# A hybrid decoder step on one core: recurrent stage reordered, loops written out, first convolution tap on ScalarE

## What is computed

```python
u = x @ w_in
gate_branch, rec = u[..., :D_RNN], u[..., D_RNN:]
xc = causal_dwconv(concat([conv_buf, rec]), conv_w, conv_b)   # width 4
r = sigmoid(block_diag(xc, w_a, b_a)); i = sigmoid(block_diag(xc, w_x, b_x))
log_a = -RG_C * r * softplus(-lam)
a, mult = exp(log_a), sqrt(-expm1(2.0 * log_a))
h = scan(h[t] = a[t] * h[t-1] + mult * i * xc)
y = (h * gelu(gate_branch)) @ w_out
```

## Time and profile before

| | us |
|---|---|
| median of 3 executions | 2996.12 (2994.41 to 3001.76) |
| profiled execution, its own time | 2997.21 |
| its span, first to last instruction | 2995.4 |
| granted TensorE clock, mean over the span | 0.955 of full speed |
| PE busy, DVE busy, POOL busy, ACT busy | 2764.8, 1695.7, 867.5, 519.7 |

### The profile page before, as it was taken

The page is one execution under the profiler, slowest core; times in us unless marked ns, Lnnn a source line. Parts: engine busy times, 40 slices in busy tenths (PEclk is TensorE's granted clock), DMA queues, the critical chain, the costliest instruction groups (busy, mean ns, idle before and its releaser), DMA issues. The chain is left out here.

```text
span 2995.4 us, 42944 instructions
## 1 busy us (share of the span) xinstructions
PE 2764.8 (92%) x16822; PEld 2682.6 (90%) x16822; DVE 1695.7 (57%) x2451; ACT 519.7 (17%) x841; POOL 867.5 (29%) x672
## 2 busy tenths in 40 slices
PE   6797999999999999999998888879999999999996
PEld 5697999999999999989996767779999999999995
DVE  7666366555556556731315656654765556555666
ACT  4335020000000000210103444431100000000001
POOL 2334233333333333323231010013333333333331
PEclk9899999999999999999997787879999999999998
DMA  5511111111111111123112212121111111111111
GB/s 140 88 49 56 37 43 43 49 44 43 43 43 50 43 43 43 56 93 129 72 56 85 82 67 88 39 99 43 43 50 43 43 43 43 49 44 43 43 50 64
DMA packets 44760, 174.04 MB, mean 58 GB/s; under 512 B 5205, under 2 KB 5781, under 8 KB 44214
## 3 DMA queue, kind: packets, MB, share of 16 engines
q1 hardware_dynamic: 39442, 143.08, 14.1%
q10 hardware_dynamic: 5156, 28.58, 3.4%
HBM read 140.20 MB, written 23.05 MB: 55 GB/s over the span
## 5 line engine op out<-in xcount | busy, mean ns | idle before, releaser
L591 PE MATMUL psum<-xn_hi,w_hi 128*128 128x352 f32 x3648 | 799.0, 327 | 70.3 <-DVE xn_lo L1246 22.9
L591 PE MATMUL psum<-xn_lo,w_hi 128*128 128x352 f32 x3648 | 791.1, 324 | 0.7 <-issue 0.7
L591 PE MATMUL psum<-xn_hi,w_lo 128*128 128x352 f32 x3648 | 789.5, 325 | 0.0
L591 PEld LDWEIGHTS psum<-xn_hi,w_hi 128*128 128x128 f32 x3648 | 624.9, 190 | 80.5 <-issue 62.1
L591 PEld LDWEIGHTS psum<-xn_lo,w_hi 128*128 128x128 f32 x3648 | 630.0, 189 | 1.8 <-issue 1.8
L591 PEld LDWEIGHTS psum<-xn_hi,w_lo 128*128 128x128 f32 x3648 | 623.1, 189 | 0.0
L530 POOL TENSOR_TENSOR carriers<-eps 128x1 f32<-128x1 f32 x208 | 63.6, 306 | 1776.2 <-PE psum L591 1636.2
L535 POOL TENSOR_TENSOR w_lo<-w_raw,w_hi 128x1024 fp32r<-128x1024 f32 x208 | 534.1, 2568 | 17.3
L1253 DVE TENSOR_TENSOR x<-psum,x 128x1056 f32<-128x1056 f32 x208 | 261.4, 1257 | 251.4 <-PE psum L591 248.9
L1205 DVE TENSOR_TENSOR line<-psum,inverse_rms 128x704 f32<-128x704 f32 x104 | 92.6, 890 | 399.5 <-PE psum L591 398.2
L1032 ACT ACTIVATE line<-line 128x1056 f32<-128x1056 f32 x48 | 52.3, 1089 | 1404.6 <-DVE line L1194 1404.6
(11 more groups left out here) (189 smaller groups left out, 2250.5 us busy)
## 6 DMA issues: line engine op xcount, KB each, us to landing
w_raw<-in_w SPq DMA_DIRECT2D x208, 512.0 KB, 3.3
k_pages<-in_cache_k SPq DMA_DIRECT2D x16, 512.0 KB, 4.4
v_pages<-in_cache_v SPq DMA_DIRECT2D x16, 512.0 KB, 5.5
scratch_line<-bias_line ACTq DMA_DIRECT2D x1, 4608.0 KB
x<-in_x ACTq DMA_DIRECT2D x8, 528.0 KB, 9.9
scratch_x<-x ACTq DMA_DIRECT2D x1, 4224.0 KB, 11.5
out_k<-k_t ACTq DMA_DIRECT2D x1, 4224.0 KB, 12.7
out_v<-line ACTq DMA_DIRECT2D x8, 528.0 KB, 2.7
```

What stands on the lines that cost most here:

```text
L591: last = pe.matmul(PS[:, 3 * (a % 2) + c, 0:CH], w[:, s, k, :], r[:, c * CH:(c + 1) * CH], start=start and first, stop=stop and final)
```

## The change

In the recurrent stage, the block-diagonal weights go into small buffers of their own (`GRAW`, `GHI`, `GLO`), loaded by own DMAs of 128 KB, so that there are 16 weight units and not 24. PE does the `rec` units of tiles 0 and 1 side by side while the first norm's inputs arrive, then norm sum, bias line and the block products of tile 0 (`diag`), and then for n = 2 to 7: rec unit n, gate unit n-2, block products n-1. The last gate unit follows the last block products. DVE and ACT are reordered with it; the scan writes straight into `Y`, which is multiplied by the gelu in place; the high and low parts of `y` tiles 0 to 6 are made before and during the last gate unit. There are two buffers for xc.

Everywhere: the first tap of each convolution (with its bias) is done by ACT, with a wait for it on DVE; every `Fori` is a Python loop; POOL's tiny additions are gone. The norm sum does the 1024 prompt columns first, waits for their root, then the 32 sample columns into bank 6, and waits for their root too. The bias line goes to DRAM once as one row per head, and a DRAM-to-DRAM DMA, issued by ACT when the last high part of `y` is made, spreads it 128-fold.

Numbering, SP and POOL:

```diff
+def acc_rec(n):
+    return n if n < 2 else 4 * n - 4
+def acc_gate(n):
+    return 4 * n + 5 if n < 6 else (28, 31)[n - 6]
+def acc_diag(n):
+    return 2 if n == 0 else 4 * n + 2 if n < 7 else 29
+def unit_rec(n):
+    return n if n < 2 else 2 * n - 2
+def unit_gate(n):
+    return 2 * n + 3 if n < 6 else n + 8
...
+            def load_gates(n):
+                if n >= 2:
+                    sp.wait_ge(g_lo, n - 1)
+                sp.dma_start(GRAW[:, n % 2], I["gates"][n]).then_inc(g_in[n % 2], 16)
+            load_weights(0, 0)
             sp.dma_start(COL[:, :], I["columns"]).then_inc(c_in, 16)
-            load_weights(0, 0)
             load_weights(1, 1)
-            pairs(2, U_O)
+            load_gates(0)
+            load_gates(1)
+            for n in range(2, KT):
+                pairs(unit_rec(n), unit_rec(n) + 1)
+                load_gates(n)
+                pairs(unit_gate(n - 2), unit_gate(n - 2) + 1)
+            pairs(unit_gate(KT - 2), U_OUT)
+            pairs(U_OUT, U_O)
...
+            straight(0, 2)
+            gates(0)
+            for n in range(2, KT):
+                straight(unit_rec(n), unit_rec(n) + 1)
+                gates(n - 1)
+                straight(unit_gate(n - 2), unit_gate(n - 2) + 1)
+            gates(KT - 1)
+            straight(unit_gate(KT - 2), U_OUT)
```

PE, one norm sum and the orders of the recurrent stage:

```diff
                 pe.matmul(PS[:, 6, :], ONES[:, :], Z[2][:, 0:512], start=True, stop=True)
                 pe.matmul(PS[:, 7, :], ONES[:, :], Z[2][:, 512:SEQ], start=True, stop=True
                           ).then_inc(sum_mm, 1)
                 pe.wait_ge(root_done, 2 * r + 1)
+                pe.matmul(PS[:, 6, 0:TS], ONES[:, :], Z[2][:, SEQ:T], start=True, stop=True
+                          ).then_inc(sum_mm, 1)
+                pe.wait_ge(root_done, 2 * r + 2)
...
+                for c in range(2):
+                    last = pe.matmul(PS[0:NH, 6 + c, :], TAB[:, :], HOT[:, c * 512:(c + 1) * 512],
...
+            def diag(n):
+                pe.wait_ge(g_lo, n + 1)
+                pe.wait_ge(xcl_ready, n + 1)
                 for g in range(2):
-                    wait_room(pe, a + 2 + g, i, 8)
-                    product((u + 2) % 2, g, a + 2 + g, XCH[:, :], XCL[:, :], True, True
+                    a = acc_diag(n) + g
+                    wait_room(pe, a)
+                    product(n % 2, g, a, XCH[:, :], XCL[:, :], True, True, GHI, GLO
                             ).then_inc(acc_done, 1)
...
+            for k in range(KT):
+                pe.wait_ge(nlo_done, k + 1)
+                for j in range(2):
+                    if k == 0:
+                        pe.wait_ge(w_lo, j + 1)
+                    last = product(j, k, acc_rec(j), XNH[:, k, :], XNL[:, k, :], k == 0, k == KT - 1)
+                    if k == KT - 1:
+                        last.then_inc(acc_done, 1)
+            norm_sum(0)
+            bias_line()
+            diag(0)
+            for n in range(2, KT):
+                unit(unit_rec(n), acc_rec(n))
+                unit(unit_gate(n - 2), acc_gate(n - 2))
+                diag(n - 1)
+            unit(unit_gate(KT - 2), acc_gate(KT - 2))
+            diag(KT - 1)
+            unit(unit_gate(KT - 1), acc_gate(KT - 1), release=True)
+            for k in range(KT):
+                pe.wait_ge(nlo_done, KT + k + 1)
+                for j in range(2):
+                    if k == 0:
+                        pe.wait_ge(w_lo, U_OUT + j + 1)
+                        wait_room(pe, A_OUT + j)
+                    last = product(j, k, A_OUT + j, XNH[:, k, :], XNL[:, k, :], k == 0, k == KT - 1)
+                    if k == KT - 1:
+                        last.then_inc(acc_done, 1)
```

ACT:

```diff
-                act.activation(RINV[:, SEQ:T], PS[:, 3, 0:TS], ACT.Sqrt, bias=EPSC[:, :],
-                               scale=1.0 / D).then_inc(root_done, 1)
-                act.wait_ge(sum_mm, 2 * r + 2)
                 act.activation(RINV[:, 0:SEQ].rearrange("p (b t) -> p b t", b=2), PS[:, 6:8, :],
                                ACT.Sqrt, bias=EPSC[:, :], scale=1.0 / D).then_inc(root_done, 1)
+                act.wait_ge(sum_mm, 2 * r + 2)
+                act.activation(RINV[:, SEQ:T], PS[:, 6, 0:TS], ACT.Sqrt, bias=EPSC[:, :],
+                               scale=1.0 / D).then_inc(root_done, 1)
...
-                act.dma_start(S["line"].rearrange("h (p i) -> h p i", p=P),
-                              BLN[:, :].unsqueeze(1).to_broadcast([NH, P, LINE])
-                              ).then_inc(line_out, 16)
+                act.wait_ge(dve_const, 3)
+                act.dma_start(S["row"], BLN[:, :]).then_inc(row_out, 16)
...
+                wait_read(act, acc_rec(n))
+                act.wait_ge(rec_state, n + 1)
+                m = SEQ + NB * (RW - 1 + NS)
+                act.activation(Z[6][:, 0:m], Z[4][:, 0:m], ACT.Identity, scale=col(C_RGW + n),
+                               bias=col(C_RGB + n)).then_inc(rec_tap, 1)
+            def xc_high(n):
+                if n:
+                    wait_acc(act, acc_diag(n - 1) + 1)
                 act.wait_ge(xc_ready, n + 1)
-                act.activation(XCH[:, :], Z[0][:, 0:T], ACT.Copy).then_inc(xch_ready, 1)
...
+                act.activation(XCH[:, :], XCS[n % 2][:, 0:T], ACT.Copy).then_inc(xch_ready, 1)
+            def gelu(n):
+                wait_read(act, acc_gate(n))
                 act.activation(Z[5][:, 0:T], Z[5][:, 0:T], ACT.Gelu_apprx_tanh
                                ).then_inc(gel_ready, 1)
...
+            def recurrence(n):
+                wait_acc(act, acc_diag(n))
+                if n < KT - 1:
+                    act.wait_ge(xc_ready, n + 2)
+                act.activation(as_acc(Z[6][:, 0:T]), acc(acc_diag(n)), ACT.Tanh, scale=0.5,
+                               bias=HBA[:, n:n + 1]).then_inc(acc_free[acc_diag(n) % 2], 1)
+                wait_acc(act, acc_diag(n) + 1)
+                act.wait_ge(h_done, n + 1)
+                act.activation(as_acc(Z[1][:, 0:T]), acc(acc_diag(n) + 1), ACT.Tanh, scale=0.5,
+                               bias=HBX[:, n:n + 1]).then_inc(acc_free[(acc_diag(n) + 1) % 2], 1)
+                wait_read(act, acc_diag(n))
+                act.activation(Z[2][:, 0:T], Z[6][:, 0:T], ACT.Tanh, scale=SP2[:, n:n + 1],
+                               bias=SP2[:, n:n + 1]).then_inc(s_ready, 1)
...
+            def y_high(k):
+                act.wait_ge(y_done, k + 1)
+                act.wait_ge(xn_free, k + 1) if k < KT - 1 else wait_acc(act, acc_gate(KT - 1))
                 act.activation(XNH[:, k, :], Y[:, k, :], ACT.Copy).then_inc(nhi_done, 1)
+            tap(0)
+            xc_high(0)
+            tap(1)
+            recurrence(0)
+            xc_high(1)
+            for n in range(2, KT):
+                tap(n)
+                gelu(n - 2)
+                recurrence(n - 1)
+                xc_high(n)
+            gelu(KT - 2)
+            recurrence(KT - 1)
+            for k in range(KT - 1):
+                y_high(k)
+            gelu(KT - 1)
+            y_high(KT - 1)
+            act.wait_ge(row_out, 16)
+            act.dma_start(S["line"].rearrange("h (p i) -> p h i", p=P),
+                          S["row"].unsqueeze(0).to_broadcast([P, NH, LINE])).then_inc(line_out, 16)
...
+                            a = up_acc(a0, g, 2 * t + v)
+                            wait_read(act, a, i, 24)
+                            act.wait_ge(q["u_state"], val(n + 1, i, 8))
+                            if f:
+                                act.wait_ge(q["gc_ready" if v else "vc_ready"], val(f, i, 4))
+                            w = C_FW + l * NFC + v * FT + f
+                            w0, wb = (col(w + j * 2 * FT, None if i is None else i * 4)
+                                      for j in (0, FW))
+                            m = SEQ + NB * (FW - 1 + NS)
+                            act.activation(TMP[v][:, 0:m], Z[4 + v][:, 0:m], ACT.Identity,
+                                           scale=w0, bias=wb).then_inc(q["tap_done"], 1)
```

DVE:

```diff
-                step(dve.tensor_scalar(tmp[:, 0:n], src[:, 0:n], taps[0], bias, MUL, ADD))
+                if bias is not None:
+                    step(dve.tensor_scalar(tmp[:, 0:n], src[:, 0:n], taps[0], bias, MUL, ADD))
...
+            def rec(n):
+                XC = XCS[n % 2]
+                dve.wait_ge(rec_used, n + 1)
+                evac_line(acc_rec(n), REC, RW - 1)
+                dve.wait_ge(rec_tap, n + 1)
+                taps = [col(C_RGW + j * KT + n) for j in range(RW)]
+                conv_first(REC, S_, taps, None, RW - 1)
                 conv_last(REC, S_, XC, taps, RW - 1, xc_ready)
...
+            def gate(n):
+                if n:
+                    dve.wait_ge(y_done, n)
+                evac(acc_gate(n), G_[:, 0:T])
+            def gated_y(n):
+                dve.wait_ge(gel_ready, n + 1)
+                dve.wait_ge(h_done, n + 2)
```

(52 more changed lines are left out.)

236 lines of the change are left out of this document (85 added, 151 removed).

## The result

The changed kernel takes 2919.8 us (median of 4 runs, 2919.4 to 2921.4) where the kernel before, run beside it, took 2996.9 (4 runs): a ratio of 0.9742, 95% interval 0.9730 to 0.9755, 77 us less. I had forecast 2909.5 with a range of 2888 to 2940. The forecast that it gets faster was right, the range held the time, and the forecast itself was 10 us too low.

What follows compares the result with a forecast made beforehand. PE, busy 92% of the span, was taken as the bound, so changes count by its standing time. Terms -42.2 + 7.8 - 26.0 - 9.2 - 17.0 = -86.6 from 2997.2 gave 2910.6, adjusted to 2909.5 us; range 2888 to 2940.

Steps and rivals of the forecast that it cites:

- Recurrent stage: Recurrent stage: 27.0 us rounds, no 16.13 us wait, third output unit at 287.2 instead of 329.43: -42.2 us.
- Start: Recurrent stage, beginning: units 0 and 1 in pairs, tile 0 read at 48.9, its block products at 58.8 us, as before.
- First round: Recurrent stage: 5.3 us of block products at the low clock, then PE waits 3.1 for ACT's first tanh, until 67.1.
- End: Recurrent stage, from 229.1 us: last gate unit to 259.5, 16.13 wait gone, new 2.2 wait, third output unit at 287.2.
- Norm sums: Norm sums: PE waits for two roots, +2.4 us for each of three in the middle, +0.6 at the end: +7.8.
- First tap in the ConvFFN: ConvFFN: tap on ACT starts the addition 0.9 us earlier, 24 times, plus 0.2 static waits, 22 times: -26.0 us.
- Loops: Loops written out: eight ConvFFN returns of 1.15 us go, -9.2; two attention returns of 8.5 go, -17.0.
- A: Rival, recurrent stage: the spread clogs the weight loads, all 24.3 us lost, 2934 us; chance 0.08.
- B: Rival, recurrent stage: DVE sets the round, rounds of 28.5 and start 3 us later, 2922 us; chance 0.15.
- C: Rival, ConvFFN: the tap on ACT gains nothing, +21.6, 2931 us, or in a worse form 2948; chance 0.14.
- D: Rival, whole kernel: straight code isn't fetched in time, 132 us of PE stalls, 3042 us; chance 0.03.
- E: Rival: A with C, and the returns' time comes back as data waits, 2986 us, nearly no change; chance 0.02.

Runs made afterwards that it cites:

- e9: Kernel before with only the spreading transfer changed to the row form (one DRAM row, spread from there), at the old place: 2976.5 us, ratio 0.9928.
- e10: Kernel before with the row form of the spread and every loop written out: 2940.2 us, ratio 0.9806.
- e7: Changed kernel with norm sums 1 to 3 back in the old order: 2912.1 us, ratio 0.9713 to the kernel before.
- e5: Changed kernel with the ConvFFN's first taps back on DVE: 2936.7 us, ratio 0.9795 to the kernel before.
- e3: Kernel before with DVE's loops alone written out: 2974.5 us, ratio 0.9922.
- e1: Kernel before with every counted loop of every engine written out, nothing else changed: 2961.1 us, ratio 0.9878.
- e2: Kernel before with PE's loops alone written out: 2989.2 us, ratio 0.9972.
- e6: Changed kernel with the spreading transfer issued early, ahead of the recurrent rounds: 2920.9 us, ratio 0.9747 to the kernel before.
- e11: Changed kernel with norm sums 1 to 3 in old order and DVE's first down-product addition ahead of the last line's taps: 2897.7 us, ratio 0.9671.
- e4: Kernel before with the old-form spreading transfer issued behind the recurrent stage instead of ahead of it: 2988.5 us, ratio 0.9974.

## Why the prediction was right, and where it was off

**Sum.** Predicted -86.6, measured -75.9 between the two profiled spans and -77.0 between medians. The mechanism was right in the main; the miss of 10.7 lies in two terms. By the stages of the table, forecast and measured: up to n1 -42.2 and -36.3, attention -17.0 and -11.2; the rest, ConvFFNs, projections and tail, -27.4 and -28.4. The experiments give the parts: loops 35.3 and form of the spread 21.7 (together 58.0), ConvFFN taps 16 to 17, POOL's tiny additions some 3 (24 times 0.13), norm order minus 8.8; what remains of the 77, 8 to 9, I put down to the new order of the recurrent stage with its small gate buffers, which no run took out alone.

**Recurrent stage, -42.2; measured -34.8.** The mechanism was right: rounds of 27.0 forecast, 27.2 measured, no 16 us wait, a new 2.2. The steps that failed are "Start", "First round" and "End". Block products of tile 0 at 60.42 instead of 58.8; a wait of 4.2 for the tanh instead of 3.1, so the next unit at 69.69 instead of 67.1; the first round 29.46 instead of 27.0, its first matmuls at 1.22 per three, the low clock; five rounds of 0.2 more; and 1.4 at the end, where the clock was low again behind the second output unit's wait (0.88 per three at 268.96). Together 7.4. Some 2 to 3 of it were this one execution: the five other runs with this order have the block products at 58.6 to 59.2, so "Start" was right up to there. What fails in all of them is the wait for the tanh (3.65 to 4.8), a first round of 28.6 to 28.7, and the end. The granted clock was 0.62 from 60.40 to 75.00 and 0.72 from 268.90 to 275.00. Of the gain, the form of the spread made 23.3 (third unit at 306.11 in e9), the loops 4.3 (301.83 in e10), and the new order 7.2 (294.65), 9 to 10 by the five other runs. The last is less than the 16.13 that I saw go, for the reason in e10. I had not split the forecast so: more than half of this term came from the spread, whose price I had put at nothing by the nearest row and not by a measurement.

**Norm sums, +7.8.** For the three in the middle I had 7.2; e7 gives 8.8, 8.2 by the table: right. For the end of the kernel I had 0.6; the tail behind the last norm's first matmul is 0.8 longer.

**First tap in the ConvFFN, -26.0.** Right. 24 x 0.9 was for the tap with POOL's earlier end: measured 0.82 and 0.13 a group, 17.4 us (e5) and some 3 (by difference). 22 x 0.2 was for the static waits: e3 shows them in every group. The inherited block was forecast to last 1.15 beyond POOL's end and lasted 1.13. The rule of the Trainium skill, "Perfetto Trace Analysis", section "Optimizing Scalar/DVE Operations", holds for the operation and not for this place: alone the tap is shorter on DVE (0.84 us at its shortest in the kernel before, L1185), but there it took 2.61 and on ACT 1.29. The page goes on that offloading "may make sense" when DVE is saturated; DVE was busy 57%, and it paid because of one block on one path.

**Loops, -9.2 and -17.0.** With the 4.4 of static waits, counted under the tap, I had 13.6 in the ConvFFNs; e1 gives 15.4. In attention I took 8.5 us per return from one head with a return and one without. That is the term that was mis-sized. Pairs of heads went from 100.60 and 102.34 us to 94.07 and 96.06, 6.5 and 6.3. The heads with a return did gain 8.3 each (54.55 to 46.21, 56.25 to 47.96), but the heads behind them became 1.8 and 2.0 longer (46.05 to 47.86, 46.09 to 48.10): they had been short at a higher granted clock. The first of these, before and then changed (columns as in e2):

```profile
1788.70:1834.75 46.05, 41.55 (x272) 35.35 (x272) 29.90 (x113) 23.12 (x54) 6.87 (x5) 0.85 0.22 80
```

```profile
1734.48:1782.34 47.86, 43.14 (x271) 36.95 (x272) 31.40 (x113) 23.08 (x54) 6.76 (x4) 0.82 0.21 78
```

The same work takes 1.6 us more of PE's busy time. The rest of the shortfall in attention is not the change: from the first 512-column score product to its last value products, the first head took 49.81 us in the changed kernel's execution against 46.99 before, and 45.11 to 48.21 in e5, e6, e7 and e11, which have the same attention code.

**Rest.** The spread was forecast to cost nothing where it is now; e6 and its 19.8 us agree. It is the form that made it so: in the old form it cost at either place (e4).

**The rivals.** A (the spread still clogs) fell: POOL waits for no weight between 282 and 400 us. B (rounds of 28.5) fell with rounds of 27.2. C (no gain from the tap) fell, with e5. D (straight code is not fetched in time) fell: over 39,213 instructions PE's idle time has "issue" only twice, 3.1 and 1.4 us. That the sequencer runs ahead is what the Trainium skill, "Runtime: NRT & Kernel Launch", section "Instruction fetch mechanics", says of such code. E (next to no gain) fell with 77 us.
